# Normalised sections that begin on unscaled tiles, an earlier decay projection, one run of transpositions and equal branch halves in a two-layer decoder trunk

## The reference, cut to what matters

```python
def rms_norm(x, g):
    y = xf * lax.rsqrt(jnp.mean(xf * xf, axis=-1, keepdims=True) + RMS_EPS)
    return (y * g)
def swiglu(x, w_gate, w_up, w_down):        # D_FF = 2816
    return (silu(x @ w_gate) * (x @ w_up)) @ w_down
def hybrid_mixer(h, ...):
    z = h @ w_in + b_in
    log_alpha = log_sigmoid(a_lr @ gla_w_alpha + gla_b_alpha) / 16
    o_a = rms_norm(gla_chunked(a_q, a_k, a_v, log_alpha)) * silu(a_r)
    o_b = nsa_attention(...)
    h_c = mlstm_chunked(...) * sigmoid(c_o)
    y = sum over branches of sigmoid(gate_b) * (o_b @ w_branch[b])
    return y @ w_out
```

## Time and profile before

| | us |
|---|---|
| median of 3 runs | 3009.97 (3009.7 to 3010.14) |
| the profiled execution | 3013.37 |
| its span in the trace | 3011.2 |
| TensorE busy | 2782.7 (92%) |
| GpSimd busy | 1062.6 (35%) |
| mean granted TensorE clock | 0.967 |

### The profile page before, as it was taken

How to read it: one execution, slowest core, us unless ns; L and a number is a source line. 1 busy time by engine, 2 the same in 40 slices (tenths; PEclk the granted TensorE clock), 3 DMA queues, 4 the chain that set the end, 5 groups by cost and what they waited for, 6 DMA issues and landing times.

```text
span 3011.2 us, 36649 instructions
## 1 busy us (share of the span) xinstructions
PE 2782.7 (92%) x13140; PEld 2181.8 (72%) x13140; DVE 1165.1 (39%) x1434; ACT 1054.5 (35%) x1525; POOL 1062.6 (35%) x449
## 2 busy tenths in 40 slices
PE   6999989999878888999989999899989888899998
PEld 4888867766656676888868888667666666678887
DVE  3332223445456333332233322244453562343322
ACT  3222223555454433222132221244554544332221
POOL 2444434312222233444334443343122222334443
PEclk9999999999998999999999999999998899999999
DMA  3223223211111122223222232132111111222222
GB/s 139 97 92 110 91 70 105 84 43 34 61 41 45 63 87 77 98 98 110 86 75 98 98 110 86 70 105 85 39 43 42 53 43 63 84 84 98 98 105 76
DMA packets 36014, 239.76 MB, mean 80 GB/s; under 512 B 3904, under 2 KB 5056, under 8 KB 13888
## 3 DMA queue, kind: packets, MB, share of 16 engines
q1 hardware_dynamic: 34336, 236.57, 22.3%
q10 hardware_dynamic: 1568, 1.72, 0.2%
HBM read 235.13 MB, written 2.10 MB: 79 GB/s over the span
## 4 chain that ended last, share of the span: by engine, by line
issue 62%; POOL 22%; PE 14%; POOLq 1%; DVE 0%; ACT 0%; DVEq 0%; ACTq 0%
POOL wlo L263 22%; PE bank L1089 5%; PE bank L1091 5%; PE bank L1090 5%; POOLq L262 1%; POOLq L258 1%; DVE hlo L663 0%; DVE ylo L1052 0%; ACT whi L294 0%; ACT L321 0%; ACT tmp L334 0%; DVE tmp L652 0%; DVE x L687 0%; DVE y L732 0%; DVE x L1062 0%
## 5 line engine op out<-in xcount | busy, mean ns | idle before, releaser
L263 POOL TENSOR_TENSOR wlo<-raw,whi 128x1024 fp32r<-128x1024 f32 (+2 forms) x440 | 1061.5, 2414 | 1929.2 <-ACT whi L285 923.4
L1089 PE MATMUL bank<-hhi,whi 128*128 128x512 f32 x2368 | 968.6, 409 | 80.1 <-DVE hlo L663 44.0
L1090 PE MATMUL bank<-hlo,whi 128*128 128x512 f32 x2368 | 937.3, 396 | 0.0
L1091 PE MATMUL bank<-hhi,wlo 128*128 128x512 f32 x2368 | 937.3, 396 | 0.0
L1089 PEld LDWEIGHTS bank<-hhi,whi 128*128 128x128 f32 x2368 | 454.8, 192 | 213.5 <-issue 92.2
L285 ACT ACTIVATE whi<-raw 128x1024 fp32r<-128x1024 f32 (+1 forms) x256 | 289.4, 1130 | 788.5 <-PE bank L1091 788.1
L1091 PEld LDWEIGHTS bank<-hhi,wlo 128*128 128x128 f32 x2368 | 453.7, 192 | 98.0
L1090 PEld LDWEIGHTS bank<-hlo,whi 128*128 128x128 f32 x2368 | 455.5, 192 | 87.8 <-issue 2.7
L675 DVE TENSOR_TENSOR tmp<-tmp,bank 128x512 f32<-128x512 f32 x88 | 60.5, 688 | 597.4 <-PE bank L1091 597.4
L1089 PE MATMUL bank<-uhi,whi 128*128 128x512 f32 x704 | 274.4, 390 | 0.0
L1091 PE MATMUL bank<-uhi,wlo 128*128 128x512 f32 x704 | 273.9, 389 | 0.0
(11 more groups left out here) (250 smaller groups left out, 2576.0 us busy)
## 6 DMA issues: line engine op xcount, KB each, us to landing
raw<-gu SPq DMA_DIRECT2D x88, 1024.0 KB, 4.7
raw<-dn SPq DMA_DIRECT2D x32, 1408.0 KB, 6.0
raw<-cb SPq DMA_DIRECT2D x48, 768.0 KB, 4.3
raw<-pM SPq DMA_DIRECT2D x16, 1024.0 KB, 4.8
raw<-cq SPq DMA_DIRECT2D x16, 1024.0 KB, 4.7
raw<-pA SPq DMA_DIRECT2D x12, 1024.0 KB, 4.7
raw<-wo SPq DMA_DIRECT2D x8, 1024.0 KB, 4.8
x<-xT SPq DMA_DIRECT2D x1, 2048.0 KB, 8.5
```

The source lines that it names most:

```text
L263: pool.tensor_tensor(wlo[:, s, 0:w], raw[:, j, lo:lo + w], whi[:, s, 0:w].bitcast(f32), ALU.subtract).then_inc(sem["lo_done"], 1)
L1089: mm(outp, wh, mhi, start=start and k == 0, stop=False)
L1090: mm(outp, wh, mlo, start=False, stop=False)
L1091: i = mm(outp, wl, mhi, start=False, stop=stop and k == len(parts) - 1)
```

## The change

**Normalised sections.** While dn and wo run, VectorE also multiplies each finished x tile by the next norm's gain, without rstd, and splits it into `hhi` and `hlo` (`pre_split`). The section's first four tiles (two units) multiply these unscaled parts at once; the sum of squares is multiplied in the middle of the second tile; VectorE scales the four results by rstd afterwards (`late`). Meanwhile x\*gain\*rstd is formed into eight new tiles `fs`, rounded by ScalarE into `hhi` as the fourth tile passes each k, and subtracted into `hlo` for the fifth tile. In gu0 and gu1 the first two units get their silu and product inside `norm`. `cur` for the next layer is loaded in gu1; its first load, x (in four pieces) and the constants are issued by ScalarE, and the table `sel` is built on the core.

**Branches.** Both tiles of a unit have 6 steps (768 wide): six gate steps, then two gate steps and four branch steps. The sigmoid is taken after the second tile. In cb2, `yhi` and `ylo` are made by unit.

**mLSTM and GLA.** The four score tiles are added on VectorE and multiplied once by ones. The decay projection goes to the last block of NSA, the GLA value transpositions to those of the mLSTM.

```diff
-WIDTHS = {... "cb": (KD * P, 4 * P)}
+WIDTHS = {... "cb": (6 * P, 6 * P)}
-CB = (..., [12 * (i // 2) + (12 if i % 2 else 8) for i in range(2 * KD)])
+CB = (..., [6 * (i + 1) for i in range(2 * KD)])
```

ScalarE (`norm`, abridged; `split_tile` calls order it):

```diff
-                    split_tile(begins, 0)
-                    split_tile(begins, 1)
-                    A(tmp[:, 5], bank[4][:], ACT.Ln, bias=eps[:, 0:1]).then_inc(sem["ln_ready"], 1)
-                    A(tmp[:, 4], tmp[:, 5], ACT.Exp, scale=-0.5).then_inc(sem["rstd_ready"], 1)
-                    for k in range(KD):
-                        act.wait_ge(sem["hf_ready"], me.at("hf_ready", f * KD + k + 1))
-                        A(hhi[:, k], tmp[:, 2 + k % 2], ACT.Copy).then_inc(sem["hhi_ready"], 1)
+                    split_tile(begins, 0)
...
+                    split_tile(begins, 1)
...
+                    split_tile(begins, 2)
+                    A(fs[:, KD - 1], bank[4][:], ACT.Ln, bias=eps[:, 0:1]).then_inc(sem["ln_ready"], 1)
+                    A(tmp[:, 4], fs[:, KD - 1], ACT.Exp, scale=-0.5).then_inc(sem["rstd_ready"], 1)
+                    split_tile(begins, 3)
+                    split_tile(begins, 4)
+                    for k in range(KD):
...
+                        A(hhi[:, k], fs[:, k], ACT.Copy).then_inc(sem["hhi_ready"], 1)
+                    split_tile(begins, 5)
+                    if f != 1:
+                        for j in range(2):
+                            act.wait_ge(sem["scaled"], me.at("scaled", 4 * f + j + 1))
+                            A(tmp[:, j], tmp[:, j], ACT.Silu).then_inc(sem["silu_ready"], 1)
+                        act.wait_ge(sem["uhi_ready"], me.at("uhi_ready", f // 2 * KF + 2))
```

VectorE:

```diff
+                def pre_split(f, c):
+                    gain = par("norm", (f + 1) % 3 * KD + c)
+                    dve.tensor_scalar(hhi[:, c], x[:, c], gain, None, ALU.mult).then_inc(sem["pre_hi"], 1)
+                    dve.wait_ge(sem["pre_hi"], me.at("pre_hi", f * KD + c + 1))
+                    dve.scalar_tensor_tensor(hlo[:, c], x[:, c], gain, hhi[:, c].bitcast(f32),
+                                             ALU.mult, ALU.subtract).then_inc(sem["pre_lo"], 1)
...
+                    for k in range(KD):
+                        dve.scalar_tensor_tensor(fs[:, k], x[:, k], par("norm", f * KD + k), tmp[:, 4],
+                                                 ALU.mult, ALU.mult).then_inc(sem["fs_ready"], 1)
+                    late(0)
+                    for k in range(KD):
+                        dve.wait_ge(sem["hhi_ready"], me.at("hhi_ready", f * KD + k + 1))
+                        dve.tensor_tensor(hlo[:, k], fs[:, k], hhi[:, k].bitcast(f32), ALU.subtract
+                    late(1)
...
+                    dve.tensor_copy(tmp[:, 4, 0:P], dm[0][:, 0:P]).then_inc(sem["dve_step"], 1)
+                    dve.tensor_tensor(tmp[:, 4, P:S], dm[0][:, P:S], dm[1], ALU.add).then_inc(sem["dve_step"], 1)
+                    dve.tensor_tensor(tmp[:, 4, 2 * P:S], tmp[:, 4, 2 * P:S], dm[2], ALU.add).then_inc(sem["dve_step"], 1)
+                    dve.tensor_tensor(tmp[:, 4, 3 * P:S], tmp[:, 4, 3 * P:S], dm[3], ALU.add).then_inc(sem["den_sum"], 1)
```

TensorE:

```diff
+                def normed_section(f, name):
+                    u = FIRST[name]
+                    tile(2 * u, 0, bank[0][:], hp, free=u - 1, ready=("pre_lo", (f - 1) * KD))
+                    for k in range(KD):
+                        step(2 * u, 1, bank[1][:], hp, k)
+                        if k == KD // 2 - 1:
+                            pe.wait_ge(sem["sum_part"], me.at("sum_part", (f + 1) * KD))
+                            mm(bank[4][:], onesm[:], tmp[:, 4], start=True, stop=True).then_inc(sem["ss_ready"], 1)
+                    tile(2 * u + 2, 0, bank[2][:], hp, free=u)
+                    tile(2 * u + 2, 1, bank[3][:], hp, passed="late_k")
+                    section(name, hp, hp, ready=("hlo_ready", f * KD), first=1)
...
-                    for jt in range(NB):
-                        i = mm(bank[6][:, jt * P:S], ones[:], dm[jt], start=jt == 0, stop=jt == NB - 1)
+                    pe.wait_ge(sem["den_sum"], me.next("den_sum"))
+                    mm(bank[6][:], ones[:], tmp[:, 4], start=True, stop=True).then_inc(sem["den_mm"], 1)
```

The last branch, ScalarE (`turn`) and VectorE:

```diff
-                    A(whi[:, 0, 0:KD * P], raw[:, 1 - j, 0:KD * P], ACT.Copy).then_inc(sem["hi_done"], 1)
+                    w = KD * P if last else 6 * P
+                    A(whi[:, 0, 0:w], raw[:, 1 - j, 0:w], ACT.Copy).then_inc(sem["hi_done"], 1)
+                    act.wait_ge(sem["tile_done"], me.at("tile_done", 2 * u + 2))
+                    A(whi[:, 1, 0:w], raw[:, 1 - j, w:2 * w], ACT.Copy).then_inc(sem["hi_done"], 1)
                     act.wait_ge(sem["y_ready"], me.at("y_ready", 2 * KD + c - 1))
                     A(tmp[:, j], bank[2 * j][:], ACT.Sigmoid, bias=par("gbias", c + 2 * KD)).then_inc(sem["gate_ready"], 1)
-                    A(whi[:, 1, 0:w], raw[:, 1 - j, KD * P:KD * P + w], ACT.Copy).then_inc(sem["hi_done"], 1)
...
+                with dve.Fori(1, KD // 2) as i:
                     for j in range(2):
                         combine_unit(2, j, FIRST["cb2"] + j + 2 * i, 2 * i + j)
+                        y_low(2 * i + j - 2)
+                for k in (KD - 2, KD - 1):
+                    y_low(k)
```

More of the change, by code:

```diff
@@ L351, in _ @@
                 norm(0)
-                section("gu0", silu)
+                section("gu0", silu, first=1)
                 split_tile("dn0", 0)
                 split_tile("dn0", 1)
-                section("dn0", down_square(0))
-                x_square("dn0", 0, KD - 1, 1)
+                section("dn0", down_square())
                 norm(1)
-                section("pA")
+                section("pA", first=1)
                 split_tile("pM0", 0)
@@ L1093, in step, with tile @@
                         i.then_inc(sem["tile_done"], 1)
-                def tile(T, s, outp, parts, free=None, start=True, stop=True, ready=None):
+                    elif passed:
+                        i.then_inc(sem[passed], 1)
+                def tile(T, s, outp, parts, free=None, start=True, stop=True, ready=None, passed=None):
                     for k in range(len(parts)):
-                        step(T, s, outp, parts, k, free, start, stop, ready)
-                def section(name, a, b, one=False, ready=None, started=False):
-                    def unit(i, j, ready=None, started=False):
+                        step(T, s, outp, parts, k, free, start, stop, ready, passed)
@@ L1103, in unit, with section @@
+                def section(name, a, b, one=False, ready=None, first=0):
+                    def unit(i, j, ready=None):
                         u = FIRST[name] + j + 2 * i
-                        if not started:
-                            tile(2 * u, 0, bank[2 * j][:], a, free=u - 1, stop=not one, ready=ready)
-                        second = ready if started else (ready[0], ready[1] + len(a)) if ready and one else None
+                        tile(2 * u, 0, bank[2 * j][:], a, free=u - 1, stop=not one, ready=ready)
+                        second = (ready[0], ready[1] + len(a)) if ready and one else None
@@ L1107, in unit @@
                         tile(2 * u, 1, bank[2 * j + (not one)][:], b, start=not one, ready=second)
-                    peel = ready is not None or started
-                    if peel:
-                        unit(0, 0, ready, started)
+                    if ready is not None:
+                        unit(first, 0, ready)
                         pe.sem_inc(sem["held"], 1)
-                        unit(0, 1)
-                    with pe.Fori(int(peel), dict(SECTIONS)[name] // 2) as i:
+                        unit(first, 1)
+                        first += 1
@@ L1124, in fill, with gated_section, unit @@
                         u, s = FIRST[name] + T // 2, T % 2
-                        step(2 * u, s, bank[2 * (u % 2) + s][:], parts[s], c - (ends[T - 1] if T else 0),
-                             free=u - 1 if s == 0 else None)
+                        gated(2 * u, u % 2, s, c % 6, free=u - 1 if s == 0 else None)
+                def gated_section(name, ready):
+                    def unit(i, j, ready=None, started=False):
+                        u = FIRST[name] + j + 2 * i
+                        for s in range(int(started), 2):
+                            for k in range(6):
+                                gated(2 * u, j, s, k, free=u - 1 if s == 0 else None, ready=ready)
+                    unit(0, 0, ready, True)
+                    pe.sem_inc(sem["held"], 1)
+                    unit(0, 1)
+                    with pe.Fori(1, dict(SECTIONS)[name] // 2) as i:
+                        for j in range(2):
+                            unit(i, j)
                 hp = [(hhi[:, k], hlo[:, k]) for k in range(KD)]
@@ L1312, in _ @@
                     values(m)
[L1314 removed]
+                for n in range(8):
                     if n >= 2:
```

400 lines of the change are left out of this document (235 added, 165 removed).

## The result

| | before | changed |
|---|---|---|
| median, us | 3010.05 (3009.7 to 3010.38, 4 runs) | 2913.25 (2910.37 to 2915.71, 4 runs) |
| the profiled execution | 3013.37 | 2915.71 |
| its span | 3011.2 | 2913.9 |

The ratio is 0.9678, with a 95% interval from 0.9661 to 0.9695: 3.2% faster. The forecast was 2918 us, in a range from 2888 to 2952. One execution of the kernel before, timed later beside e1 to e4, took 6712.8 us and is not used.

The account below looks back on a forecast made before the run. TensorE was taken as the bound, busy 2782.7 of 3011.2 us, with time to win only at joints and in the mixer. Joints -36.2 and mixer -55.4 summed to -91.6, giving 2918 us as median, range 2888 to 2952.

Parts of the forecast that it names:

- Joint into pA: Between dn0 and pA's third tile, both layers: cost falls from 14.3 to 7.1 us, -7.2 each.
- first stall 2.2: In pA's fifth tile: TensorE waits 2.2 us for the first `hlo` subtraction, delayed by GpSimd's weight splits.
- Joint into gu1: Into gu1, both layers: joint costs 8.4 us, seventh tile's weights late because ScalarE is held; -5.9 each.
- into layer 1's gu0: Joint into layer 1's gu0: squares come after dn1, so the sum is late; 11 us against 18.0, -7.0.
- Start: Program's start: first step at 18.5, third tile at 34.5 against 44.55, minus 7.1 for the re-split; -3.0 us.
- Ahead of the mLSTM: Before the mLSTM, per layer: log-sigmoid ends, scalings and `selr` fills lengthen VectorE's convolution chain; +3.4 us.
- lead-in: mLSTM to GLA, per layer: transposed-tile wait goes, wait at GLA's level grows from 1.6 to 4.5; -9 us.
- Heads: mLSTM heads, per layer: denominator products fall from 2.07 to 0.83 us, -1.2 by four heads; -4.9 us.
- cb2 and wo: Per layer: six-step tiles cover the weight splits in cb2 (-11.1), wo's wait shrinks (-3.7); -14.8 us.
- (B): Rival for the joints: the re-split hides between VectorE's operations, six joints win about 5 us each; 2890 us, chance 0.12.
- (C): Rival for the mixer: waits move instead of going, giving back 24 us; 2942, to 2955 us; chance 0.23.
- (D): Rival: slower, since short idles at joints cost three extra slow-clock tiles each; 3016 us or more, chance 0.02.

Follow-up runs that it names:

- e1: Changed kernel with the four denominator products per mLSTM head restored and VectorE's adds of the score tiles removed; 2919.3 us.
- e4: Changed kernel with the weights of cb1's first two tiles copied before cb0's last sigmoid; 2912.8 us.
- e2: Changed kernel with rstd copied to a PSUM bank, from which the eight `fs` products read it; 2900.3 us.
- e3: Changed kernel with ScalarE copying the seventh tile's weights before its wait for the second product of gu0 and gu1; 2898.3 us.
- e7: Changed kernel with ScalarE copying the first weights without waiting for x, and waiting for each piece of x ahead of its square; 2911.9 us.
- e5: Changed kernel with three of eight cb0 steps moved ahead of an mLSTM head's wait for the previous head's output; 2887.2 us.
- e10: Changed kernel with the edits of e5 and e1 together; 2896.7 us.
- e6: Changed kernel with branch units cut into 8 and 4 steps again and the sigmoid after the gate tile, in all three branches; 2931.8 us.
- e8: e4 with VectorE also making the mLSTM's low parts before the decay's two scans; 2912.3 us.
- e9: Changed kernel with the edits of e2, e3, e5 and e8 together; 2859.9 us.

## Why the prediction was right, point by point

**Right in the whole**, 4.8 us above the median, with errors of both signs inside: by the table, some stages won 20 us more than forecast and others 14 less. That the sum came this close is in part luck; most of the places and mechanisms came as written.

- *Joint into pA, -7.2.* It was -10.7: 3.7 us are left, not 7.1. Order and causes came as written, and e2 shows the blocking by GpSimd to be the cause. The terms "first stall 2.2" and "second stall 2.2" were over-sized, since a stall is the difference of two long chains: `fs` ended 0.8 us sooner than walked through, the scalings took 0.4 less and the tile came 0.2 later, together the 1.4 that the first stall lacks. The second was 1.4, two steps further on. The term "another 1.5 to 2 us" for the clock was wrong at this place: over the joint it stayed at 1.00.
- *Joint into gu1, -5.9; into layer 1's gu0, -7.0.* Measured -6.7 and -7.3, but by other parts. In gu1 the part up to the sixth tile cost 3.7, and the seventh tile 4.4 with the clock; the mechanism for the latter (ScalarE held for the second product) was forecast and e3 shows it. In gu0 the late squares cost 7.1, of which the forecast had 2.2 as a wait, and the re-split with the seventh tile 3. Squares during dn1 were not tried.
- *Start, -3.0.* Measured -2.7. First step 20.7 instead of 18.5, third tile 35.1 instead of 34.5. e7 shows why an error of two microseconds in the first hardly reached the second. The 7.1 taken for the re-split was 6.8 by other parts: e3 shows 3.6 of them at the seventh tile, which the forecast walked through for gu1 only.
- *Ahead of the mLSTM, +3.4.* Measured +5.3 and +6.4. From the last NSA block's end to the first head it is +3.6 in layer 0, as forecast; the other 1.8 us are the two decay products on TensorE, now in the last block, where they delay it. They were taken out of the lead-in and put in nowhere. The lead-in won 13.1 to 13.6 instead of 10.2: the wait at GLA's first level is 2.44 us where 4.5 was forecast.
- *Heads, -4.9.* The step that failed. Measured, with the last denominator, about -2.3 for both layers together where -9.8 was forecast. It took 1.24 us by four as a saving of time, but part of the heads runs at half clock behind the waits, and that part grew from 42 to 81 matmuls. e1, e5 and e10 show it: the same four products cost 6 us where slow spells are there to be spared, and 9.4 where they are not.
- *cb2 and wo, -14.8.* Measured -16.2 and -16.0, with units of 8.16 us against 8.2 forecast. e6 shows the halves to be the cause in cb2. The even cut also moved the clock in the heads, for the worse by 2.7 and 4.2 us in the two layers, which no term had.
- *Rivals.* (B), no blocking, is refuted by the rows of `fs`, though each joint into pA came to within 2.2 us of it. (C) was true of the heads only. (D) is refuted: the longest slow stretch of a joint is half a tile.
- The tests named: joints between 3 and 10 (3.7 into pA, 8.1 into gu1; 10.7 into layer 1's gu0, which is over the limit of 10, though the forecast itself had 11 there), cb2 units under 9, no wait inside a feed-forward section, 3.5 us at cb1's first step for "about 4". The wait ahead of the mLSTM's first head did not grow in layer 0 (1.8 for 2.8 us) and grew in layer 1 (3.4 for 2.8); the longer chain shows in waits of the transpositions before it.

## What to carry to other kernels

A short wait of TensorE can be dearer than it reads: look at the pitch of the matmuls behind it, and lay work that is ready over the wait before making the work around it shorter. Where VectorE and GpSimd overlap on the critical path, putting one operand of VectorE's operation in PSUM costs a copy and takes the blocking away. A wait's length says nothing of its worth until it is known which chain ends next: 3.5 and 4.6 us of waits were removed here for nothing, while four waits of about 2 us at the seventh tiles gave 15.

## What was not expected of the hardware

- Behind a wait of 1.8 us TensorE ran 6 to 13 matmuls at 1.2 GHz (0.43 us apart instead of 0.23) in most heads, but not in all: in the kernel before, heads 2 and 4 of layer 0 and head 2 of layer 1 have the same wait of 1.79 us and no slow matmul behind it. What decides between the two is open. With the wait gone, no head behind the first had more than one slow matmul (e5, e10, e9).
- That an edit elsewhere moves it: e3 and e8 leave the heads' code as it is, and their heads took 80.4 to 85.1 us where 83.8 and 85.2 stood. Differences of some microseconds between variants can therefore be clock and not work, and the windows have to be read. The five executions of e3, e4 and e7 spread by 10, 11 and 21 us, and their mean granted clock goes with the time: e7 took 2896.5 us at 0.985 and 2917.3 at 0.978. Only one execution of each was profiled, so where in the kernel this happens is not shown.
